# Around two attentions: first scores released by one bank half, first k step of the next product moved between the last tiles

## What is computed

```python
# first block, second layer: window attention (16 heads, 4 KV heads, d = 64)
x = x + gate * ((window_attention(q, k, v, k_ctx, v_ctx, sink) * silu(g)) @ w_out_c)
# second block: causal attention with a forget gate beside a depthwise convolution
attn = fox_attention(q, k, v, log_f)                       # 8 heads, d = 64
u = silu(layer_norm(causal_depthwise_conv(conv_val * sigmoid(conv_gate))))
y = concatenate([attn, u], -1) @ w_o
x = x + g1 * rms_norm(y)
```

## Time and profile before

| | |
|---|---|
| time, median of 3 runs | 2511.76 us (2510.68 to 2514.68) |
| span of the profiled execution | 2521.1 us |
| PE / DVE / ACT / POOL busy | 92% / 57% / 31% / 55% |
| mean granted TensorE clock | 0.963 |

### The profile page before, as it was taken

How to read it: one execution, slowest core, us unless ns; L and a number is a source line. 1 busy time by engine, 2 the same in 40 slices (tenths; PEclk the granted TensorE clock), 3 DMA queues, 4 the chain that set the end, 5 groups by cost and what they waited for, 6 DMA issues and landing times. The chain is left out here.

```text
span 2521.1 us, 32205 instructions
## 1 busy us (share of the span) xinstructions
PE 2317.9 (92%) x11283; PEld 1911.4 (76%) x11283; DVE 1435.2 (57%) x2162; ACT 773.5 (31%) x1405; POOL 1390.9 (55%) x1372
## 2 busy tenths in 40 slices
PE   6898999899999999989878988999999999999995
PEld 2687888788878777867746767777788878888874
DVE  1653646668793699964679878848612222222136
ACT  3321112123220688842333338833310000000012
POOL 2536553745984788536678843366755633333360
PEclk9899999999999899999989989999999999999997
DMA  7436335514456556342233476552322211111121
GB/s 276 147 95 194 105 101 174 185 52 150 150 190 199 160 167 168 101 176 84 67 109 90 142 181 169 164 209 88 92 80 72 96 43 49 47 46 51 51 67 67
DMA packets 180446, 305.92 MB, mean 121 GB/s; under 512 B 34940, under 2 KB 73528, under 8 KB 179008
## 3 DMA queue, kind: packets, MB, share of 16 engines
q1 hardware_dynamic: 140512, 222.75, 29.8%
q10 hardware_dynamic: 39776, 81.12, 8.7%
HBM read 247.14 MB, written 56.66 MB: 121 GB/s over the span
## 5 line engine op out<-in xcount | busy, mean ns | idle before, releaser
L1165 PE MATMUL PS<-HXH,WH 128*128 128x512 f32 (+1 forms) x1904 | 761.2, 400 | 72.3 <-DVE MOD L2206 25.5
L1046 POOL TENSOR_SCALAR WH<-RAW 128x512 fp32r<-128x512 f32 (+1 forms) x466 | 341.4, 733 | 818.5 <-PE PS L1167 671.2
L1166 PE MATMUL PS<-HXL,WH 128*128 128x512 f32 (+1 forms) x1904 | 751.7, 395 | 0.0
L1167 PE MATMUL PS<-HXH,WL 128*128 128x512 f32 (+1 forms) x1904 | 750.8, 394 | 0.0
L1049 POOL TENSOR_TENSOR WL<-RAW,WH 128x512 fp32r<-128x512 f32 (+1 forms) x466 | 630.7, 1354 | 38.9
L1165 PEld LDWEIGHTS PS<-HXH,WH 128*128 128x128 f32 (+1 forms) x1904 | 362.1, 190 | 160.5 <-DVE MOD L2206 27.6
L1167 PEld LDWEIGHTS PS<-HXH,WL 128*128 128x128 f32 (+1 forms) x1904 | 361.5, 190 | 80.1 <-issue 2.1
L1166 PEld LDWEIGHTS PS<-HXL,WH 128*128 128x128 f32 (+1 forms) x1904 | 362.6, 190 | 78.7 <-issue 3.6
L2430 DVE TENSOR_TENSOR TM<-PS,TM 128x512 f32<-128x512 f32 x44 | 28.3, 686 | 380.9 <-ACT TM L1849 380.9
L1849 ACT ACTIVATE TM<-PS 128x512 f32<-128x512 f32 x44 | 23.9, 595 | 556.6 <-PE PS L1167 556.6
L2443 DVE TENSOR_TENSOR Y<-PS,Y 128x2048 f32<-128x2048 f32 x40 | 91.7, 2292 | 123.8 <-PE PS L1167 123.7
(11 more groups left out here) (313 smaller groups left out, 4124.7 us busy)
## 6 DMA issues: line engine op xcount, KB each, us to landing
RAW<-in_ada_w SPq DMA_DIRECT2D x160, 256.0 KB, 2.7
RAW<-in_w_ffn_in SPq DMA_DIRECT2D x224, 128.0 KB, 2.1
RAW<-in_w_in_ab SPq DMA_DIRECT2D x88, 256.0 KB, 2.6
RAW<-in_w_in SPq DMA_DIRECT2D x56, 256.0 KB, 2.6
RAW<-in_w_ffn_out SPq DMA_DIRECT2D x56, 256.0 KB, 2.6
XR<-XX ACTq DMA_DIRECT2D x3, 4096.0 KB, 12.1
XX<-XR ACTq DMA_DIRECT2D x3, 4096.0 KB, 14.0
RAW<-in_w_in_c SPq DMA_DIRECT2D x40, 256.0 KB, 2.6
```

The source lines that it names most:

```text
L1046: g.tensor_scalar(WH[:, sw, 0:m], RAW[:, r, 0:m], 1.0, 0.0, ALU.mult, ALU.add).then_inc(gpsimd_done, 1)
L1165: mm(out, wh, xh, start=first, stop=False, **kw)
L1166: mm(out, wh, xl, start=False, stop=False, **kw)
L1167: return mm(out, wl, xh, start=False, stop=last, **kw)
```

## The change

It does these things:

1. PE waits before the first scores of each attention for banks 0 to 3 only, and for 4 to 7 before the first tile. ACT's waits at the start of both attentions go.
2. In `attf`, the sums `cvar` are multiplied at step 2 on PE, their Sqrt is done on ACT behind the Exp of step 3, and DVE's reciprocals of it start at step 7 and not 5. The low halves of V (`h1`) are stored by SP, behind the loads for head 1 and ahead of the load of V.
3. The high and low parts of some k tiles for the next product's h0 are made within the last steps (`high_rows`, `low_rows`), and the k step that comes first is multiplied there, 6 of its 12 matmuls at each of two steps (`lin_step`). For `("wo", 0, "h0")` the k order becomes 7, 6, 5, 4, 0, 1, 2, 3. The rows of `HXL` are kept in reversed order.
4. In `attc`, the gating of the last block of outputs (`gated(7)`, L2156 before) comes behind DVE's low parts for h0.

```diff
-CONV_TAIL = (5, 7, 9, 11, 13, 15, 17, 19, 22)
+CONV_TAIL = (7, 9, 11, 13, 14, 15, 17, 19, 22)
+WO_FIRST = [7, 6, 5, 4, 0, 1, 2, 3]
...
-            return (HXL if lo else HXH)[:, k, off:off + n]
+            return HXL[:, KT - 1 - k, off:off + n] if lo else HXH[:, k, off:off + n]
...
+        CO_STARTS = (131, 132)
+        WO_STARTS = {71: (0, (0, 1)), 72: (0, (2, 3))}
...
                 if f == 8:
-                    load_v(0)
                     load_qk(1)
                     load_nb(1)
+                    store_v_low()
+                    load_v(0)
...
+            def lin_step(e, at_, js):
+
+                n, k = e["ws"][at_], (e["ks"] or range(KT))[at_] if "ks" in e else at_
+                sw = WPOS[n]
+                pe.wait_ge(gpsimd_done, upto("w", n))
+                pe.wait_ge(vector_done, upto("H", *HMAKER[e["layer"]], e["part"], k))
+                for j in js:
+                    ws = slice(j * P, (j + 1) * P)
+                    ins = three(bank(e["name"], j), WH[:, sw, ws], WL[:, sw, ws], hs(e["part"], k, 0), hs(e["part"], k, 1),
+                                at_ == 0, False)
+                if 3 in js:
+                    ins.then_inc(products_done, 1)
+                    did(products_done, ("used", n))
...
                 elif kind == "attc":
-                    for job_before in prev[name]:
-                        pe.wait_ge(*of("free", job_before))
+                    pe.wait_ge(*of("free", prev[name][0]))
...
+                        if u == min(tiles):
+                            pe.wait_ge(*of("free", prev[name][1]))
...
+                        if u == 2:
+                            conv_sums(("cvar", "x"))
...
+            CO_HIGH = {129: [0], 132: [1], 133: [2], 134: [3]}
+            WO_HIGH = {66: [7], 68: [6], 70: [5], 71: [4]}
...
                 elif kind == "attc":
-                    for job_before in prev[name]:
-                        act.wait_ge(*of("free", job_before))
-                    act.wait_ge(products_done, upto("job", ("g", 1, "h1")))
-                    for j in range(1, 4):
-                        act.wait_ge(*of("tm", (("g", 1, "h1"), j)))
...
-                if i == 3:
+                if i == 3 and b < 7:
+                    gated(b)
...
+            CO_LOW = {129: [0], 133: [1], 134: [2, 3]}
+            WO_LOW = {71: [7], 72: [6], 73: [5, 4]}
```

More of the change, by code:

```diff
@@ L111, in lin, with weights @@
                        mid=mid, last=last, h=h, **kw))
-    def weights(layer, group, kts=KT):
-        return [slot("split", (layer, group, k), None) for k in range(kts)]
+    def weights(layer, group, ks=range(KT)):
+        return [slot("split", (layer, group, k), None) for k in ks]
     def ev(kind, name, **kw):
@@ L587, in program @@
         masks_loaded = sem("masks_loaded")
+        v_low_stored = [sem(f"v_low_stored{j}") for j in range(4)]
         q_stored = [sem(f"q_stored{j}") for j in range(4)]
@@ L936, in load_v, with store_v_low @@
                 did(v_loaded[hd % 2], ("vl", hd), by=16)
+            def store_v_low():
+                off = PARTS["h1"][0]
+                for j in range(4):
+                    sp.wait_ge(vector_done, upto("slo", ("v2", "h1"), j))
+                    sp.dma_start(VSD[off + j * P:off + (j + 1) * P, :, 1, :],
+                                 SPL[j][:, :].bitcast(F32).rearrange("p (h n) -> p h n", n=64)).then_inc(v_low_stored[j], 16)
+                    did(v_low_stored[j], ("vls", j), by=16)
             first_wo = min(n for n, x in enumerate(SLOTS) if x[1][0] == "wo")
@@ L2014, in _ @@
                         did(scalar_done, ("csq", j))
[L2015 to L2019, removed]
                 elif kind == "out":
@@ L2091, in _ @@
                             did(scalar_done, ("exp", "f", u))
+                        if u == 3:
+                            x = ("cvar", "x")
+                            act.wait_ge(products_done, upto("job", x))
+                            A(CRST[:, :].rearrange("p (b n) -> p b n", n=HALF), PS[:, 4 * setof[x]:4 * setof[x] + 2, :],
+                              ACT.Sqrt, scale=1.0 / 512, bias=EPT[:, :]).then_inc(scalar_done, 1)
+                            did(scalar_done, "csd", ("free", x))
+                        if u in WO_HIGH:
+                            high_rows(2, "h0", WO_HIGH[u])
                         for z, j in tiles.get(u, [])[2:]:
@@ L2521, in _ @@
                     n = e["n"]
-                    b = 0 if part == "h0" else 1
-                    for k in range(KT):
-                        dve.wait_ge(scalar_done, upto("lh", n, part, k))
-                        v.tensor_tensor(hs(part, k, 1), LR[b][:, k, :], hs(part, k, 0).bitcast(F32), ALU.subtract).then_inc(vector_done, 1)
-                        did(vector_done, ("H", "hload", n, part, k))
+                    low_rows(n, part, range(KT) if part == "h1" else range(4, KT) if n == 1 else range(4))
+                    if n == 1 and part == "h0":
+                        gated(7)
                 elif kind == "resid":
```

106 lines of the change are left out of this document (75 added, 31 removed).

## The result

| | before | changed |
|---|---|---|
| median | 2511.76 us (17 runs) | 2517.35 us (17 runs) |
| span of the profiled execution | 2521.1 us | 2516.1 us |

The account below looks back on a forecast made before the run. PE, busy 92% of the 2521.1 us span, was taken as the bound, through its waits on the product chain and lower clock. Terms -3.0 + 1.0 + 0 - 4.1 = -6.1 took the median 2511.76 to 2505.7 us; range 2500 to 2510.7.

Parts of the forecast that it names:

- B: Exit of the window attention: second k step 5.5 us earlier, all given back in the wait for `MOD`; 1.0 us lost.
- 4 x 0.65 = 2.6 us, by the row at 1643.56, and the gating takes 1.23: Window attention exit: DVE's time for low parts of k 4 to 7, then gating, which ends 6.0 us later.
- The landing to follow the reload: Window attention exit: h1's load lands 4.2 us later, at 1121.9, as the reload `XX` is issued 4.2 later.
- The low parts of h1 at 0.65: Window attention exit: POOL is through by about 1116, so the last two low parts cost 0.65 us each, not 1.27.
- A: Entry of the window attention: first scores near 825.5, maximum of step 4 3.3 us earlier; 3.0 us gained, bounds 1.5 to 5.
- C: Entry of the second attention: scores 5.9 us earlier, offset by `cvar` sums and ACT's table loads; 0, 2 gained to 4 lost.
- a sign of being wrong: Entry of the second attention: the forecast there is wrong if PE waits for `VS`; V expected at 1511 to 1512.
- D: Exit of the second attention: second k step at about 1645.5, not 1649.65; 4.1 us gained, bounds 2 to 5.5.
- The other edits: Reversed `HXL` rows, DVE's reciprocals two steps later, and a fulfilled POOL wait dropped: claimed to cost nothing.
- rival 1: Reload costs in full: low parts stay about 1.27 us or h1's load queues; B costs 3 to 4.2, about 2509.8; chance 0.32.
- Rival 2: Second product's wait gives way: h1's load lands as before, PE resumes 2 to 5 us earlier; about 2500 us; chance 0.12.
- Rival 3: Second attention: V lands 11 us or more after its first multiplication wants it; loss of 5, 2516.8 us; chance 0.05.
- Rival 4: Neither entry gives anything: A 0, B +1, D -4.1, or 2508.7 us; no separate chance, within own case and rival 1.

Follow-up runs that it names:

- the kernel that holds POOL back: Changed kernel, but POOL splits weights for slots of the first product only after the last gating; ratio to before 0.9989.
- A alone: Only A kept, the other three parts put back to the order of before; ratio to before 0.9985, second time 0.9996.
- three moves in one queue: Changed kernel with DVE's last gating before low parts k 4 to 7, `MOD` before the residual add, that add before h1's low parts; ratio to before 0.9933.

## Why the prediction was wrong

*B is the step that failed*, in its size and in what it left out. "4 x 0.65 = 2.6 us, by the row at 1643.56, and the gating takes 1.23" priced DVE's work without asking what POOL does in that stretch. The prediction let POOL follow the product 5.5 us earlier, and drew from it only the good half, that the low parts of h1 would be free of it. The same move puts its splits beside the low parts of h0. With 2.29 us for two, 5.16 for four and 1.52 for the gating, 3.9 us more than the 1.29, 2.50 and 1.23 of the kernel that holds POOL back, the reload was issued 7.9 us later than without B and not 4.2. "The landing to follow the reload" was right, but at 23 us. The prediction had the 22.4 of the first profile of before; in six of ten executions without B it is near 20.5, so against those B pays some 2 us more. The low parts of h1 at 0.65 came as forecast; from the last copy to `MOD` it is 4.7 us with B and about 7.3 without, 2.6 gained where the sum had 3.2. The term was +1.0 and measured +6 to +8 in the traces (7.9 and 6.2 at `MOD`, 8.3 and 7.1 in the third product), beyond its bound of 4.2. The wait grew to 17.9 us, not 13.

*A* was right: 3.3 us earlier at the maximum of step 4, as forecast, and 3.4 us in the third product (3.0). *C* was right in size as far as it can be told: 0 was taken; the Exp of step 4 came 2.0 us sooner behind `SPL`, where the prediction had it 0.45 later. PE did wait 0.94 us for V, which the prediction had named as a sign of being wrong. A load's end and the next activation are 0.02 us apart (1503.03 + 1.28 and 1504.33), so nothing beyond the 1.28 us of a table load shows. *D* gave 4.9 us in one pair of traces and 4.1 against the mean, with 4.1 forecast; with C beside it the two gave 3.4. *The other edits* cost nothing.

The rivals: rival 1, the reload at its full price, came nearest, with B at 3 to 4.2. The landing did follow the reload in full, but the slow low parts were those of h0, not of h1, and it had no term for them. Rival 2, an early landing, fell. Rival 3, V late by 11 us, fell. Rival 4 fell with A. The ratio of 1.0018 lies just inside the 0.2% that the prediction called same (0.37), on the slow side, which got 0.07 because no case had B worse than 4.2.

*The sum.* By the traces A -3.4, B +8.3, and C and D together -3.4 make +1.5, and from the mark to the end of the fourth product behind the second attention the two profiles of the changed kernel took 924.5 and 920.5 us against 924.3 and 918.7 of before: +1. The timed runs say +2.5 to +6.5. These 1 to 5 us are not located, and remain open; before timed against itself gave 1.0013, so the noise of a ratio can hold part of them. What made the profile of before 5 us longer than the changed one's lies outside the change: 4.1 us ahead of the mark and 1.7 us behind 2220. To subtract its 9.3 us excess as a constant was harmless for the sum, but it told that profiles of this kernel differ by more than what was to be forecast.

*Open:* why the load of h1 took 23 us in all eight profiles with B, where the reload itself landed late. In these a load of weights is issued 0.7 to 1.7 us behind the reload, without B none before 5.3 us. That this traffic is the cause was not tried, and four profiles without B have a late landing too.

## What to carry to other kernels

Before work is put ahead of a store or load that starts a long chain, follow that chain to the next product that waits: here the second k step came 6 us earlier and the third product 8 us later. When one engine starts earlier, list every instruction of its neighbours that it newly runs beside, not only those that it leaves. A wait that takes back a gain may be removable by order alone: `MOD`, made at 315.8 where 289.9 was possible, stood behind work that it did not need, and three moves in one queue brought the kernel from 4.5 us over before to 17 us under it.

## What the runs showed of the hardware that was not expected

DVE's low part with 128x512 elements takes 0.65 us alone and 1.29 in the mean beside POOL's splits, in either half, and the gating (128x1024) 1.23 against 1.52. POOL pays as well: its subtraction for `WL`, 1.29 us alone, takes 1.60 to 2.13. The longer time is waiting: a low part that starts during an instruction of a split ends 0.53 to 0.56 us after that instruction, in 288 of 288 cases. One and the same program has stretches with several lengths: 49.1 or 54.2 us for the same 192 matmuls ahead of the window attention (A alone, twice), and 12.5 or 14.0 us from the issue of the 4 MB reload to its landing (before, twice). Two single profiles put the changed kernel 5 us ahead of before, while the timed runs put it 4.5 us behind.
